# Scores of two heads in turn on the two halves of TensorE, softmax in eight steps, scaling on GpSimd

## The reference

```python
q = rmsnorm(q.reshape(B, T, N_HEADS, HEAD_DIM), q_gain[i])
k = rmsnorm(k.reshape(B, T, N_HEADS, HEAD_DIM), k_gain[i])
logits = q @ k.T * scale - slope[h] * (t - s)      # causal, per head
y_att = softmax(logits) @ v
h = h + concatenate([y_lru, y_att]) @ w_out[i]
```

## Time and profile before

| | |
|---|---|
| median of three runs | 665.81 us |
| profiled execution, its own time | 666.83 us |
| its span, first to last instruction | 664.9 us |
| TensorE busy | 654.8 us |
| VectorE busy | 371.5 us |
| ScalarE busy | 287.2 us |
| GpSimd busy | 319.0 us |
| DMA | 65.39 MB, mean 98 GB/s |

### The profile page before, as it was taken

One profiled execution on the slowest core, in us unless ns is written; L12 is line 12 of the kernel. 1 busy time (PEld: TensorE's weight loads), 2 busy tenths in 40 slices (PEclk: granted clock), 3 DMA queues, 4 the chain that ended last, 5 costly groups with the idle time before them and its releaser, 6 DMA issues.

```text
span 664.9 us, 8664 instructions
## 1 busy us (share of the span) xinstructions
PE 654.8 (98%) x2978; PEld 542.9 (82%) x2978; DVE 371.5 (56%) x518; ACT 287.2 (43%) x432; POOL 319.0 (48%) x232
## 2 busy tenths in 40 slices
PE   7999999999999999999999999999999999999997
PEld 5888888887888888888888888888888888888886
DVE  5682689889867677655555555555522222222464
ACT  5657653656656444433333433333422222223521
POOL 6664343703114647655555555555555554444430
PEclk9999999999999999999999999999999999999999
DMA  8633221210041314222223223322222222222211
GB/s 318 256 112 111 96 95 64 95 33 1 0 159 54 115 54 158 95 95 95 95 95 101 98 100 99 105 97 95 95 96 96 95 95 95 95 95 96 79 63 48
DMA packets 20181, 65.39 MB, mean 98 GB/s; under 512 B 2368, under 2 KB 3008, under 8 KB 20160
## 3 DMA queue, kind: packets, MB, share of 16 engines
q1 hardware_dynamic: 19584, 64.57, 28.6%
q10 hardware_dynamic: 576, 0.53, 0.2%
HBM read 62.99 MB, written 2.10 MB: 98 GB/s over the span
## 4 chain that ended last, share of the span: by engine, by line
PE 92%; DVE 3%; ACT 2%; issue 1%; DMA 1%; ACTq 0%; DVEq 0%
PE bank L958 29%; PE bank L959 29%; PE bank L960 29%; PE bank L996 1%; ACT prob L475 1%; DVE prob L789 1%; PE bank L999 1%; PE bank L1004 1%; PE bank L1106 1%; DVE prob L801 1%; DMA raw<-in_weights 1%; PE bank L1092 1%; PE bank L1054 1%; DVE prTlo L837 0%; ACT prThi L489 0%
## 5 line engine op out<-in xcount | busy, mean ns | idle before, releaser
L298 POOL TENSOR_TENSOR wlo<-raw,whi 128x512 fp32r<-128x512 f32 x106 | 142.5, 1344 | 315.9 <-ACT whi L331 315.9
L331 ACT ACTIVATE whi<-raw 128x1024 fp32r<-128x1024 f32 x106 | 111.8, 1057 | 228.0 <-PE bank L960 227.9
L958 PE MATMUL bank<-uhi,whi 128*128 128x512 f32 (+1 forms) x496 | 192.5, 388 | 0.0
L960 PE MATMUL bank<-uhi,wlo 128*128 128x512 f32 (+1 forms) x496 | 191.3, 386 | 0.0
L959 PE MATMUL bank<-ulo,whi 128*128 128x512 f32 (+1 forms) x496 | 191.3, 386 | 0.0
L299 POOL TENSOR_TENSOR wlo<-raw,whi 128x512 fp32r<-128x512 f32 x106 | 164.9, 1556 | 0.0
L958 PEld LDWEIGHTS bank<-uhi,whi 128*128 128x128 f32 x496 | 93.2, 188 | 19.5 <-issue 0.7
L959 PEld LDWEIGHTS bank<-ulo,whi 128*128 128x128 f32 x496 | 93.2, 188 | 19.4 <-issue 0.7
L960 PEld LDWEIGHTS bank<-uhi,wlo 128*128 128x128 f32 x496 | 93.2, 188 | 18.6
L892 DVE SCALAR_TENSOR_TENSOR tmp<-tmp,vec 128x511 f32<-128x511 f32 (+1 forms) x48 | 64.8, 1349 | 27.9 <-ACT tmp L537 24.8
L958 PE MATMUL bank<-acthi,whi 128*128 128x512 f32 x192 | 74.7, 389 | 0.0
(11 more groups left out here) (184 smaller groups left out, 834.8 us busy)
## 6 DMA issues: line engine op xcount, KB each, us to landing
raw<-in_weights SPq DMA_DIRECT2D x106, 512.0 KB, 3.3
res<-in_x_t SPq DMA_DIRECT2D x8, 256.0 KB, 7.3
xtok<-in_x SPq DMA_DIRECT2D x4, 512.0 KB, 9.6
out<-fin SPq DMA_DIRECT2D x7, 256.0 KB, 2.0
raw<-in_weights SPq DMA_DIRECT2D x6, 256.0 KB, 8.0
gw<-in_gates SPq DMA_DIRECT2D x1, 512.0 KB, 12.7
ptok<-in_p_t SPq DMA_DIRECT2D x1, 512.0 KB, 3.4
raw<-in_weights ACTq DMA_DIRECT2D x2, 128.0 KB, 5.5
```

Source lines behind the costliest of these rows:

```text
L298: nc.gpsimd.tensor_tensor(wlo[s][:, 0:CW // 2], raw[s][:, 0:CW // 2], whi[s][:, 0:CW // 2].bitcast(F32), ALU.subtract)
L331: nc.scalar.activation(whi[s][:, :], raw[s][:, :], ACT.Copy).then_inc(w_hi, 1)
L958: mm(o, ahi, bhi, start=start, stop=False)
L960: return mm(o, alo, bhi, start=False, stop=stop)
```

## The change

- The softmax goes by eight steps, two for each pair of heads. An even step has the 512-column tiles of both heads and the 256-column tile of the first; an odd step has the 384- and 128-column tiles of both and the 256-column tile of the second. Each step has 1280 columns, as a head had.
- Within a step, matmuls of equal tiles of the two heads are issued in turn: term by term, first head (rows 0 to 63), second head (rows 64 to 127), into different banks.
- DVE's logits take the minimum of the negated value, and the exponential has scale -1, so the negation is gone; each exponential waits for its own part.
- GpSimd multiplies `prob` by the reciprocals, which DVE still makes (`sums`).
- `prob` has four buffers. Three score steps and three fills stand before the loop; in the loop it is scores of h+3, exponentials and reciprocals of step h+2.
- The transposes of a head wait until both steps of its pair are scaled.
- The attention share of the output projection is dealt out differently: two key pairs in each of iterations 5 and 6, the third pair for two weight chunks in iteration 7.

```diff
-SCORES = [(3, 4, 0), (2, 5, 0), (0, 5, 384), (1, 6, 0)]
+SCORES = ([((0, 3, 4, 0), (1, 3, 5, 0)), ((0, 1, 6, 0),)],
+          [((0, 2, 4, 0), (1, 2, 5, 0)), ((0, 0, 4, 384), (1, 0, 5, 384)), ((1, 1, 6, 0),)])
+STEPS = 2 * PAIRS
-        prob = [at(f"prob{i}", [P, S_COLS], BIG + (48 + 5 * i) * KB) for i in range(2)]
+        prob = [at(f"prob{i}", [P, S_COLS], BIG + off * KB) for i, off in enumerate((48, 53, 8, 68))]
...
+            def normalise(st):
+
+                pool.wait_ge(rinv_ok, st + 1)
+                for n, (e, i, _, _) in enumerate(parts(st)):
+                    v = prob[(2 * (st // 2) + e) % 4][:, S_OFF[i]:S_OFF[i] + (i + 1) * P]
+                    nc.gpsimd.tensor_scalar(v, v, sm[:, st % 2, 15 + n:16 + n], None, ALU.mult).then_inc(prob_ok, 1)
+
+            normalise(0)
+            normalise(1)
+            for h in range(HEADS):
+                if h + 2 < STEPS:
+                    normalise(h + 2)
+                if h in (1, 2, 4, 6):
+                    lo_part(C_OA + h // 2, h // 2)
...
-                act.wait_ge(nmax_ok, h + 1)
-                for i, _, _ in SCORES:
-                    v = prob[h % 2][:, S_OFF[i]:S_OFF[i] + (i + 1) * P]
-                    nc.scalar.activation(v, v, ACT.Exp, bias=sm[:, h % 2, 4 + i:5 + i],
-                                         accum_out=sm[:, h % 2, 8 + i:9 + i]).then_inc(exp_ok, 1)
+                for n, (e, i, _, _) in enumerate(parts(st)):
+                    v = prob[(2 * (st // 2) + e) % 4][:, S_OFF[i]:S_OFF[i] + (i + 1) * P]
+                    act.wait_ge(logit_ok, parts_upto(st) + n + 1)
+                    nc.scalar.activation(v, v, ACT.Exp, bias=sm[:, st % 2, n:n + 1], scale=-1.0,
+                                         accum_out=sm[:, st % 2, 10 + n:11 + n]).then_inc(exp_ok, 1)
...
-                V.tensor_scalar(sm[:, h % 2, 4:8], sm[:, h % 2, 0:4], -1.0, None, ALU.mult).then_inc(nmax_ok, 1)
-
-            def normalise(h):
-                dve.wait_ge(exp_ok, 4 * (h + 1))
-                V.reciprocal(sm[:, h % 2, 12:16], sm[:, h % 2, 8:12]).then_inc(rinv_ok, 1)
-                dve.wait_ge(rinv_ok, h + 1)
-                for i, _, _ in SCORES:
-                    v = prob[h % 2][:, S_OFF[i]:S_OFF[i] + (i + 1) * P]
-                    V.tensor_scalar(v, v, sm[:, h % 2, 12 + i:13 + i], None, ALU.mult).then_inc(prob_ok, 1)
+            def sums(st):
+                dve.wait_ge(exp_ok, parts_upto(st + 1))
+                k = len(parts(st))
+                V.reciprocal(sm[:, st % 2, 15:15 + k], sm[:, st % 2, 10:10 + k]).then_inc(rinv_ok, 1)
...
+            def scores(st):
+
+                p = st // 2
+                if st:
+                    pe.wait_ge(logit_ok, parts_upto(st))
+                    pe.wait_ge(qkT_lo, PAIRS + p + 1)
+                for group in SCORES[st % 2]:
+                    for term in range(3):
+                        for e, i, b, c0 in group:
+                            if st == 0 and term == 0:
+                                pe.wait_ge(qkT_lo, PAIRS + b - 3)
+                            r, w = slice(DH * e, DH * (e + 1)), (i + 1) * P
+                            q = (qkThi, qkTlo, qkThi)[term][0][r, p, i * P:w]
+                            k = (qkThi, qkThi, qkTlo)[term][1][r, p, 0:w]
+                            last = mm(bank[b][:, c0:c0 + w], q, k, start=term == 0, stop=term == 2)
                 last.then_inc(s_done, 1)
...
-                pe.wait_ge(prob_ok, 4 * (h + 1))
+                pe.wait_ge(prob_ok, parts_upto(2 * (h // 2 + 1)))
...
-            scores(0)
-            out_lru(0)
-            scores(1)
-            out_lru(1)
+            for st in range(3):
+                scores(st)
+                out_lru(st)
             pe.wait_ge(v_lo, TT)
             for h in range(HEADS):
                 turn_probs(h)
-                if h + 2 < HEADS:
-                    out_lru(h + 2)
+                if h + 3 < KD:
+                    out_lru(h + 3)
+                elif h < HEADS - 1:
+                    out_att(h - 5, (0, 1))
                 else:
-                    out_att(h + 2 - HEADS, (0, 1, 2))
+                    out_att(0, (2,))
+                    out_att(1, (2,))
                 values(h)
-                if h + 2 < HEADS:
-                    scores(h + 2)
+                if h + 3 < STEPS:
+                    scores(h + 3)
```

More of the change, by code:

```diff
@@ L159, in build @@
         ssq = at("ssq", [P, 2, TT * HEADS], C0 + 1888)
-        sm = at("sm", [P, 2, 16], C0 + 2144)
+        sm = at("sm", [P, 2, 20], C0 + 2368)
         qg4 = at("qg4", [P, PAIRS], C0 + 2272)
@@ L170, in build, with parts, parts_upto @@
         hb8 = at("hb8", [P, 2 * LT], C0 + 2336)
-        assert C0 + 2336 + 32 <= 207 * KB and base[0] + 219 * KB <= nc.sbuf_usable_end
+        assert C0 + 2368 + 160 <= 207 * KB and base[0] + 219 * KB <= nc.sbuf_usable_end
+        def parts(st):
+            return [part for group in SCORES[st % 2] for part in group]
+        def parts_upto(st):
+            return sum(len(parts(i)) for i in range(st))
         bank = [ctx.enter_context(nc.psum_tensor(f"bank{i}", [P, 512], F32)) for i in range(8)]
@@ L200, in build @@
         v_hi, v_lo, qg_ok = sem("v_hi"), sem("v_lo"), sem("qg_ok")
-        s_done, logit_ok, nmax_ok, exp_ok, rinv_ok, prob_ok = (
-            sem(n) for n in ("s_done", "logit_ok", "nmax_ok", "exp_ok", "rinv_ok", "prob_ok"))
+        s_done, logit_ok, exp_ok, rinv_ok, prob_ok = (
+            sem(n) for n in ("s_done", "logit_ok", "exp_ok", "rinv_ok", "prob_ok"))
         pt_done, prT_hi, prT_lo, pv_done = (sem(n) for n in ("pt_done", "prT_hi", "prT_lo", "pv_done"))
@@ L311, in _ @@
             nc.gpsimd.tensor_tensor(gwlo[:, :, :, :], gw[:, :, :, :], gwhi[:, :, :, :].bitcast(F32), ALU.subtract).then_inc(gw_lo, 1)
-            with pool.Fori(2, N_CHUNKS // RING) as i:
+            with pool.Fori(2, C_OA // RING) as i:
+                for s in range(RING):
+                    lo_part(s + i * RING, s)
+            def normalise(st):
[10 more added lines that the diff above has]
+                    lo_part(C_OA + h // 2, h // 2)
+            with pool.Fori(C_UP // RING, N_CHUNKS // RING) as i:
                 for s in range(RING):
@@ L468, in _, with exps @@
             hi_part(23, 3)
-            def exps(h):
-                act.wait_ge(nmax_ok, h + 1)
-                for i, _, _ in SCORES:
-                    v = prob[h % 2][:, S_OFF[i]:S_OFF[i] + (i + 1) * P]
-                    nc.scalar.activation(v, v, ACT.Exp, bias=sm[:, h % 2, 4 + i:5 + i],
-                                         accum_out=sm[:, h % 2, 8 + i:9 + i]).then_inc(exp_ok, 1)
+            def exps(st):
+                for n, (e, i, _, _) in enumerate(parts(st)):
[3 more added lines that the diff above has]
+                                         accum_out=sm[:, st % 2, 10 + n:11 + n]).then_inc(exp_ok, 1)
             act.wait_ge(chunk_done, C_V + 4)
@@ L483, in _ @@
             exps(0)
+            exps(1)
             for h in range(HEADS):
@@ L489, in _ @@
                     nc.scalar.activation(prThi[:, c0:c0 + w], bank[b][:, 0:w], ACT.Copy).then_inc(prT_hi, 1)
-                if h + 1 < HEADS:
-                    exps(h + 1)
+                if h + 2 < STEPS:
+                    exps(h + 2)
                 if h in (1, 2, 4, 6):
@@ L776, in _, with logits @@
             qk_split(1)
-            def logits(h):
-                if h == 0:
+            def logits(st):
+                if st == 0:
                     dve.wait_ge(dist_ok, 1)
@@ L783, in logits @@
                     dve.wait_ge(qk_t, 2 * PAIRS)
[L784 to L787, removed]
-                    w = (i + 1) * P
[L789 to L792, removed]
-                V.tensor_scalar(sm[:, h % 2, 4:8], sm[:, h % 2, 0:4], -1.0, None, ALU.mult).then_inc(nmax_ok, 1)
-            def normalise(h):
-                dve.wait_ge(exp_ok, 4 * (h + 1))
-                V.reciprocal(sm[:, h % 2, 12:16], sm[:, h % 2, 8:12]).then_inc(rinv_ok, 1)
-                dve.wait_ge(rinv_ok, h + 1)
-                for i, _, _ in SCORES:
-                    v = prob[h % 2][:, S_OFF[i]:S_OFF[i] + (i + 1) * P]
-                    V.tensor_scalar(v, v, sm[:, h % 2, 12 + i:13 + i], None, ALU.mult).then_inc(prob_ok, 1)
+                p = st // 2
+                dve.wait_ge(s_done, st + 1)
+                if p >= 2:
+                    dve.wait_ge(pt_done, 3 * (2 * p - 2))
+                for n, (e, i, b, c0) in enumerate(parts(st)):
+                    w = (i + 1) * P
+                    V.tensor_tensor_reduce(prob[(2 * p + e) % 4][:, S_OFF[i]:S_OFF[i] + w], bank[b][:, c0:c0 + w],
+                                           dist[:, (TT - 1 - i) * P:T], -slope(2 * p + e), -3.0 * NEG, ALU.add, ALU.min,
+                                           sm[:, st % 2, n:n + 1]).then_inc(logit_ok, 1)
+            def sums(st):
+                dve.wait_ge(exp_ok, parts_upto(st + 1))
+                k = len(parts(st))
```

(35 more changed lines are left out.)

## The result

The change makes the kernel slower: 675.61 us (median, 674.04 to 677.14) against 665.85 before, a ratio of 1.0144 (95% interval 1.012 to 1.0169). The forecast was 662.7 us, its own range 661.3 to 664.6, and the range over all cases went up to 668.3. The profiled execution of the changed kernel took 674.04 us, with a span of 672.1. The four runs fall into two pairs, 674.0 and 674.2 us at a mean granted clock of 0.992, 677.0 and 677.1 at 0.990 and 0.989, and the trace is one of the faster pair.

What follows compares the result with a forecast made beforehand. TensorE, busy for 98% of the span, was taken as the bound. Scores -3.3, old gaps -2.1 and new waits +2.3 gave -3.1 us, so 662.7 us; own range 661.3 to 664.6, over the cases 660.7 to 668.3.

Steps and rivals of the forecast that it cites:

- What bounds the kernel: Whole span: TensorE, busy 98%; what the attention stage (83.4 us) gains or loses goes through to the end.
- Scores on two halves: Score matmuls: the two heads' matmuls overlap, weight loads don't; 3.2 us for a pair instead of 4.22, gain 3.3 us.
- The old gaps go: TensorE's waits for DVE in the attention stage vanish, 2.1 us without the one at the start.
- The scaling's cost on GpSimd: Scaling of probabilities: one-input rate, 0.61 us for 512 columns; 2.0 us for an odd step, 1.6 for an even one.
- New waits: TensorE before transposes: 0.3 us each at heads 2 and 4, 1.7 at head 6, 2.3 us in all.
- The slower rival: GpSimd scales at the two-input rate, delaying transposes of heads 2, 4 and 6: net +2.5 us, 668.3; chance 0.17.
- the two rivals together: Score halves don't overlap and GpSimd scales at the two-input rate: about +4.5 us, 670.3; chance 0.07.
- the halves don't overlap: Score matmuls: a pair stays at 4.22 us, net about 0, 665.8; chance 0.20.
- weight loads overlap too: Score matmuls: weight loads of both halves also run in parallel, 1.6 us less, 661.0; chance 0.13.
- GpSimd at the two-input rate: Scaling on GpSimd runs at the two-input rate (1.34 us for 512 columns): net +2.5 us, 668.3; chance 0.17.

Runs made afterwards that it cites:

- Experiment 3: The changed kernel with no scaling of the probabilities at all, the transposes waiting for the exponentials instead: 658.73 us, ratio 0.9892.
- experiment 7: The changed kernel with GpSimd's scaling replaced by a multiplication by a constant (even steps) and an in-place copy (odd steps), no normalisation: 660.38 us in one run.
- experiment 4: The changed kernel with useless matmuls ahead of the wait before the transposes of heads 0, 2, 4 and 6: 670.25 us, ratio 1.0063.
- experiment 6: The changed kernel, scaling on VectorE, first weight chunk split one iteration earlier, second head's score matmuls waiting for the first's end: 667.15 us, ratio 1.0022.
- experiment 1: The changed kernel with the scaling of the probabilities back on VectorE, all else as changed: 663.71 us, ratio 0.9967.
- experiment 10: The kernel before with only the scaling moved to GpSimd, in the same form as in the changed kernel: 679.48 us, ratio 1.019.
- experiment 2: The changed kernel with each score tile's three matmuls issued one behind another, the heads not in turn: 675.85 us, ratio 1.0144.
- experiment 11: The changed kernel, scaling on VectorE, first weight chunk split one iteration earlier, score tiles issued whole without turns: 661.24 us, ratio 0.9928.

## Why the prediction was wrong

- **What bounds the kernel, and that the stage's change goes through:** right. 92.6 - 83.4 = 9.2 us in the stage, 9.8 in the medians.
- **Scores on two halves:** the mechanism was right, the size too small. I took weight loads for a limit of their own: 3.2 us for a pair, measured 2.66. Four pairs save 6.2 us, and 5.4 without the first step's, whose time TensorE spends waiting for v (1.41 us against 0.54), as predicted. The spacing of 0.11 us in the earlier trace rows was misread: couples of 128 columns stand as far apart with two loads as single matmuls do with one, so it is no limit on loads of both halves together.
- **The old gaps go:** right for VectorE's remainders in the changed kernel, where TensorE's waits for them are gone. The 2.1 us are not measured apart. Experiment 3, where no longer wait covers them, still has one of 0.6, and its stage (76.7 us, 127.59 to 204.27) is 6.7 shorter than before: 5.4 for the scores leave 1.3 for the gaps.
- **The scaling's cost on GpSimd is the step that failed.** The prediction said "The scaling has one input tensor, so I take the first", that is 0.61 us for 512 columns from a conversion's row, with 1.28 as the upper end. Measured: 1.57. The number of inputs was the wrong key: by it the prediction put an odd step at 2.0 us. A copy does run at that rate (0.51 for 384 columns, experiment 7), a multiplication by a constant doesn't (1.49 for 512), and a product of two tensors takes 1.04. The true cost lay outside bounds drawn from rows of other operations.
- **New waits:** the chain was right, its term was not. An odd step takes 4.5 us, not 2.0, and the chain hands the 2.5 on: I had 0.3 us before heads 2 and 4, and it became 2.87 and 2.85; 1.7 before head 6 became 4.31; and head 0, which I held covered, waits 1.6. That is 11.6 us against 2.3.
- **The clock is the step that was missing.** I gave waits their length as price and the clock no term at all. Behind each of the three long ones TensorE worked at half speed for a while (granted clock 0.79, 0.79 and 0.77 in the stretches), some 5 us in all (experiment 4). The slower rival had the right place but neither this cost nor the right duration, and so ended at 668.3; even the two rivals together, at 670.3, stay 5 us under the measured time.
- **The sum again:** -5.4 for the scores, -2.1 for old gaps, +11.6 for waits, +4.6 for the clock: +8.7 us, against 9.2 in the stage; 0.5 have no place. All but the old gaps are measured. Counted from experiment 3 the gap is smaller: its 76.7 us without its own wait of 0.6, with 11.6 for waits and 4.6 for the clock, are 92.3 of 92.6.
- **The rivals:** "the halves don't overlap" falls (trace, experiment 6), and "weight loads overlap too" holds. "GpSimd at the two-input rate" was nearest, by place and size, though not by its reason: the product of two tensors is faster than that rate and the scalar form slower.

The Trainium skill (GPSIMD Engine Reference, 3.1) speaks of about 2.6 cycles an element for two-input work; no row here shows the scalar multiplication at its one-input rate, and the measured 1.57 us for 512 columns decides.

The Trainium skill (TensorEngine Tiling (Array Packing), Key Properties) has both loads and matmuls of different tiles in parallel. The couples' rows agree: 0.06 to 0.12 us from one couple of 128 columns to the next.

## What to carry to other kernels

Before moving work to an idle engine, measure that very instruction there: the form (scalar, copy, two tensors) changed its cost up to 2.5 times (384 columns: 1.25, 0.51 and 0.83 us), and rows of other operations didn't bound it. Ask who waits for the moved work; with one iteration's lead it must fit the lead of its slowest step, and here the odd steps decided while the even ones had time. Price a wait of TensorE at more than its length: in this stage a spell of slow clock behind one cost 1.5 to 1.7 us, and it came behind each wait of 2.48 us or more that a trace read here shows and behind some shorter ones (experiments 1 and 10). Read the granted clock in the stretch behind it.

## What the runs showed of the hardware that was not expected

- GpSimd: in-place multiplication by a scalar for each row takes 1.57 us for 512 columns and 0.63 for 128; by a constant 1.49; as a product with a repeated column 1.04 (0.83 for 384); a copy 0.51 for 384. Why a product of two tensors is the faster one stays open.
- TensorE's halves: matmuls on rows 0 to 63 and 64 to 127 overlap with their weight loads as far as the rows tell (a couple of 512 columns in 0.23 us, of 128 in 0.06 to 0.12), also where all three of one head are issued ahead of the other's (experiments 2 and 11).
- Clock: after waits of 2.87 and 2.85 us 512-column matmuls start 0.43 us apart for a few microseconds (mean grant of the stretch 0.79). In experiment 1 a wait of 1.75 us had the same after it (0.79), while the changed kernel's 1.61 us before head 0 did not (1.00). In experiment 10 a wait of 1.44 us had it (0.82) and one of 1.77 did not (0.99); in experiment 6 it came behind the score matmuls of the first step and a wait of 0.39 us (0.83 from 130.88 to 140.86). So the length of a wait alone doesn't decide it, and no run here shows what does.
- VectorE beside GpSimd: five multiplications take 1.41 us alone and 3.46 beside a weight subtraction of 2.5 us. Moving the subtraction by one iteration was worth 2.5 us.
